# Attention in a two-layer decoder trunk: TensorE weighs the values ahead of both turnings of a step

## The reference

```python
# mixer A: 8 heads of 64, three dilated causal windows, mixed by their softmax denominators
o_a = dilated_mixture_attention(qa, ka, va)
# mixer B: 8 heads of 96 (64 + 32 rotary), values of 64, plain causal attention
s = jnp.where(k_pos[None, :] <= q_pos[:, None], s, -jnp.inf)
p = jax.nn.softmax(s, axis=-1).astype(v.dtype)
o = jnp.einsum('bhqk,bkhd->bqhd', p, v)
return jnp.concatenate([o_a, o_b], axis=-1) @ w_out
```

## Time and profile before

| | us |
|---|---|
| median of 3 runs | 2953.01 (2952.48 to 2954.64) |
| profiled execution | 2956.97 |
| its span | 2955.0 |
| attention stage in it | 263.9 to 539.4 |
| TensorE busy, whole span | 2678.8 (91%) |
| VectorE busy | 1859.8 (63%) |
| ScalarE busy | 1623.2 (55%) |
| GpSimd busy | 605.6 (20%) |

### The profile page before, as it was taken

How to read it: one execution, slowest core, us unless ns; L and a number is a source line. 1 busy time by engine, 2 the same in 40 slices (tenths; PEclk the granted TensorE clock), 3 DMA queues, 4 the chain that set the end, 5 groups by cost and what they waited for, 6 DMA issues and landing times. The chain is left out here.

```text
span 2955.0 us, 40222 instructions
## 1 busy us (share of the span) xinstructions
PE 2678.8 (91%) x13762; PEld 2149.4 (73%) x13762; DVE 1859.8 (63%) x2137; ACT 1623.2 (55%) x2050; POOL 605.6 (20%) x498
## 2 busy tenths in 40 slices
PE   7998999987999999957999997887998899999992
PEld 6885677765888787845888885765886688888771
DVE  5335766427888888865352351666453788888885
ACT  4224555324888888854232233774122688888882
POOL 0000000001343444421000001553000333333440
PEclk9998999998999999978999998888999899999996
DMA  4315110135999999952332324763214699999994
GB/s 149 88 42 169 37 44 23 36 133 188 374 378 372 373 376 371 369 222 67 102 114 76 99 86 130 275 232 140 76 36 152 235 387 384 375 372 371 366 363 194
DMA packets 306470, 618.69 MB, mean 209 GB/s; under 512 B 31832, under 2 KB 80496, under 8 KB 306224
## 3 DMA queue, kind: packets, MB, share of 16 engines
q1 hardware_dynamic: 281456, 570.94, 54.9%
q0 software_dynamic: 19136, 33.61, 3.0%
q10 hardware_dynamic: 5760, 12.59, 1.1%
HBM read 566.55 MB, written 86.13 MB: 221 GB/s over the span
## 5 line engine op out<-in xcount | busy, mean ns | idle before, releaser
L2371 DVE TENSOR_TENSOR moe_w_low<-moes_raw,moe_w_high 128x2048 fp32r<-128x2048 f32 x384 | 868.6, 2289 | 161.8 <-ACT moe_w_high L2300 161.1
L2300 ACT ACTIVATE moe_w_high<-moes_raw 128x2048 fp32r<-128x2048 f32 x384 | 725.3, 1916 | 122.6 <-PEq L150 55.7
L2167 POOL COPY moe_pick<-moes_tokens 128x1 int32 (+1 forms) x64 | 89.6, 1399 | 597.2 <-PE moe_px L2216 596.3
L174 PE MATMUL moe_pg<-moe_w_high,moe_x_high 128*128 128x512 f32 x512 | 205.9, 402 | 3.7 <-DVE moe_x_low L2421 3.7
L174 PE MATMUL moe_py<-moe_w_high,moe_h_high 128*128 128x512 f32 x512 | 209.0, 408 | 0.0
L174 PE MATMUL moe_pu<-moe_w_high,moe_x_high 128*128 128x512 f32 x512 | 204.4, 399 | 0.0
L176 PE MATMUL moe_pg<-moe_w_high,moe_x_low 128*128 128x512 f32 x512 | 202.0, 395 | 0.0
L176 PE MATMUL moe_py<-moe_w_high,moe_h_low 128*128 128x512 f32 x512 | 201.1, 393 | 0.0
L176 PE MATMUL moe_pu<-moe_w_high,moe_x_low 128*128 128x512 f32 x512 | 200.9, 392 | 0.0
L175 PE MATMUL moe_pg<-moe_w_low,moe_x_high 128*128 128x512 f32 x512 | 200.1, 391 | 0.0
L175 PE MATMUL moe_py<-moe_w_low,moe_h_high 128*128 128x512 f32 x512 | 199.5, 390 | 0.0
(11 more groups left out here) (385 smaller groups left out, 6222.5 us busy)
## 6 DMA issues: line engine op xcount, KB each, us to landing
moes_raw<-in_w_gate SPq DMA_DIRECT2D x128, 1024.0 KB, 12.4
moes_raw<-in_w_up SPq DMA_DIRECT2D x128, 1024.0 KB, 12.7
moes_raw<-in_w_down SPq DMA_DIRECT2D x128, 1024.0 KB, 12.3
sproj_raw<-in_w_in_ssd SPq DMA_DIRECT2D x40, 512.0 KB, 4.2
comb_rows<-Y SPq DMA_DIRECT2D x32, 512.0 KB, 8.8
scan_sums<-CSR SPq DMA_DIRECT2D x7, 2048.0 KB, 14.1
XC<-sproj_c SPq DMA_DIRECT2D x24, 512.0 KB, 5.1
HN<-plan_hn SPq DMA_DIRECT2D x16, 512.0 KB, 3.0
```

The lines of the kernel that those rows point to most:

```text
L174: nc.tensor.matmul(out, lh, rh, start=start, stop=False)
L2167: nc.gpsimd.tensor_copy(pick[a][:, :], M.tokens[:, bass.ds(b, 1)]).then_inc(picked[a], 1)
L2300: nc.scalar.activation(wh[c % SPLIT_SLOTS][:, :], M.raw[j][:, :], ACT.Copy).then_inc(w_high, 1)
L2371: nc.vector.tensor_tensor(wl[j][:, :], M.raw[c % RAW_SLOTS][:, :], bits(wh[j][:, :]), ALU.subtract).then_inc(w_low, 1)
```

## The change

In TensorE's order the weighing of step s - 2 moves from between the two turnings of step s - 1 to ahead of both. The orders of the other engines, the waits, the buffers and the work stay as they were.

```diff
             for s in range(NS + 2):
                 if s < NS:
                     scores(s)
-                if 1 <= s <= NS:
-                    turn(s - 1, 0)
                 if s >= 2:
                     weigh(s - 2)
                 if 1 <= s <= NS:
+                    turn(s - 1, 0)
                     turn(s - 1, 1)
```

## The result

| | before | changed |
|---|---|---|
| median of the timed runs, us | 2953.82 (2952.48 to 2955.96) | 3001.99 (2996.6 to 3004.76) |
| profiled execution, us | 2956.97 | 3003.27 |
| its span, us | 2955.0 | 3001.4 |
| attention stage in it | 263.9 to 539.5, 275.6 | 264.7 to 587.1, 322.4 |

The changed kernel is slower by a ratio of 1.0157 [1.0145, 1.0169]. The span grows by 46.4 us. The attention stage grows by 46.8, and what lies ahead of it by 0.8. The output projection behind it takes 94.7 in place of 95.8: the clock was at its lower level for 3.4 us at its start (591.0 to 594.4), before for 6.8 (542.2 to 549.0). All that follows takes 2318.8 against 2318.9. So the change costs what it costs inside the stage, as forecast; forecast were 40 us, and 46 to 48 were measured.

What follows compares the result with a forecast made beforehand. TensorE was taken to bound the attention stage. Terms of 6.3 us per first-half pair and 3.7 per second-half pair, four of each, gave +40 us and 2993 us, within a range of 2972 to 3015.

Steps and rivals of the forecast that it cites:

- likeliest case: Whole kernel: the attention stage grows by 40 us, giving 2993 us, own range 2986 to 3000; 75 in 100.
- Two signs: Attention stage: forecast wrong if the second half loses as much as the first, or the granted clock falls inside.
- TensorE sets the pace: Attention stage: TensorE busy 121.49 of 124.00 us in the first four pairs, 149.16 of 151.40 in the last; others wait.
- Late mask, kind A: First-half pairs: next scores wait for head 1's mask behind head 0's late copy; 0.72 to 0.90 us at t = 4 to 7.
- Bank wait, kind B: Second-half pairs: head 1's turning waits for a bank head 0's copy empties; 0.68, 0.79, 0.57 us at t = 5 to 7.
- The steps t = 1 to 4 lose nothing: Second-half pairs: only the bank wait remains and head 1's mask is hidden, so these steps lose 0 us.
- ScalarE's chain at t = 0: t = 0 steps: weighing waits for ScalarE's high copy behind head 1's exponential; 1.2 us first half, 1.7 second.
- Behind the last scores: End of the attention stage: the t = 0 chain comes once more without scores, about 1.8 us.
- rival D: Attention stage: the clock falls too, a half-speed spell in each first-half pair adding 24 us, 3017; 10 in 100.
- A (the bank alone, 2973): Attention stage: only the bank stalls of head 1's turning count, 2.5 us a pair, 20 in all; 8 in 100.
- C: Whole kernel: no change, 2953 us, waits of before swapped one for one; 3 in 100.
- B: Attention stage: faster, the weighing filling waits of turnings for exponentials, 7.2 us gone, 2946; 4 in 100.

Runs made afterwards that it cites:

- e3: Changed kernel with VectorE writing head 1's mask ahead of its copy of head 0's turned tiles; 2975.18 us, ratio 1.0062.
- e4: Changed kernel with three PSUM banks for turned tiles, the weighing's two result tiles becoming one; 3013.43 us, ratio 1.0190.
- e5: Kernel before with both turnings ahead of the weighing; 2984.23 us, ratio 1.0104.
- e7: Changed kernel without the weighing's wait for the finish two steps back; 3003.96 us in one execution.
- e8: Changed kernel with ScalarE copying head 1's high tiles ahead of head 1's exponential; 2992.26 us, ratio 1.0123.
- e1: Kernel before with the weighing first only in the first half of the attention stage; 2980.77 us, ratio 1.0075.
- e2: Kernel before with the weighing first only in the second half of the attention stage; 2976.75 us, ratio 1.0070.
- e9: Kernel before with head 1's mask ahead of head 0's copy (first half, t = 0 to 4) and weighing first at t = 2 to 4; 2951.50 us, 0.9981.
- e6: Kernel before with head 1's mask ahead of head 0's copy on VectorE, first half, t = 0 to 4; 2953.17 us, ratio 0.9993.

## Why the prediction was right

The direction, the place and the three mechanisms came out as said; the size was 7 us low in 47, at 1.0157 where 2993 over 2953 is 1.0135. The measured 3001.99 is within the whole range, but just above the likeliest case's own, 2986 to 3000. The shares of the halves did not come out: forecast were 23.4 and 16.6 us, measured 24.2 and 22.6, so nearly the whole miss is in the second half. Two signs that the prediction named for being wrong are therefore met or nearly so: the second half lost almost as much as the first, and the granted clock did fall inside the stage, at 577.3. Point by point:

- **TensorE sets the pace, so new holes show in full.** Right. Work stayed the same, TensorE's share of the first half fell to 81% as forecast, and nothing outside the stage took part.
- **Late mask, kind A.** Right in sign, place and size of the steps: t = 4 to 7 forecast at 0.85, 0.90, 0.81, 0.72, measured 0.87, 0.93, 0.84, 0.84. For t = 1 to 3, my estimate of 1.8 together, measured 1.86. At t = 5 to 7 it comes last by only 0.12 to 0.24 (e3), with the bank's stall right beneath it (e4). e3 recovers some 28 us; that is more than the growth of these steps, since it removes a wait that was there before too, kind B's, and part of the chain at t = 0.
- **Bank wait, kind B.** Right, and confirmed by e4 (19.3 us of it became 1.9) and e5 (it needs only the turnings side by side). The size was off: 0.79, 0.68, 0.57 forecast for t = 5 to 7, measured 1.01, 0.85, 0.73. The term "1.43 after its turning starts" is 1.53 in the rows, since VectorE's semaphore took some 0.15 us and not 0.05. Another 0.09 is the later start of the weighing behind scores of kind B. Together 0.55 a pair, 2.2 us.
- **"The steps t = 1 to 4 lose nothing" in kind B.** The one step that failed. They lose 0 + 0.23 + 0.18 + 0.11 = 0.52 a pair, 2.1 us. I had shown head 1's mask to be hidden at t = 6, and carried it to small t, where head 0's scores and head 1's turning are too short to cover it. e3 shows the cause: with the mask early all three are back at 2.47, 3.33 and 4.21.
- **ScalarE's chain at t = 0.** Right: 1.2 and 1.7 forecast, 1.26 and 1.75 measured. e7 lets the trace name it, and e8 removes its longest part at the predicted price of one exponential less a small wait.
- **Behind the last scores.** 1.8 forecast, 3.3 measured. The clock fell there for 577.3 to 580.7, so weighing and sums took 3.48 us (577.42 to 580.90) where they took 1.90 before (532.95 to 534.85): 1.6 more.
- **The clock inside the stage.** From 277 to 577 it stayed at 1.00, with 32 bank stalls of up to 0.8 us and waits of TensorE of up to 1.1 for a maximum and 1.2 for the high copy. So rival D had no part in the changed kernel but for the one spell behind the last scores, worth 1.6 us and not 24. What the Trainium skill says in "TensorE: Matmul & The Clock Gate", section "A second HAM failure mode: psum-queue depth-cycling", did not show in this pattern of short holes. Single spells of some 3.4 us, not of the 12 I had priced, came in t = 0 steps of e1, e2 and e4 and, in the changed kernel, e2 and e7, behind the last scores, where TensorE waits 1.1 to 1.8 us at once.
- **Rivals.** A (the bank alone, 2973) is close to what e3 measured when the row maximum's wait was taken away, 2975, but in the sum only: it has 2.5 us in every pair, e3 has 1.5 in kind A and 3.1 in kind B. C fell with the result, and so did B. B was also priced too high. The 7.2 us of the earlier trace rows, and the 5.4, are idle time of weight loads (PEld), not of matmuls; TensorE's holes in the whole stage were 2.51 + 2.24 us. A gain in small steps exists (e3, e9), but needs the mask to come first.

The misses add up: 2.2 for the bank's handovers, 2.1 for the small steps of kind B, 1.5 behind the last scores, and 0.8 in kind A's four pairs (24.2 against 23.4) make 6.6, which takes the 40 to 46.6 of the 46.8 measured.

## What to carry to other kernels

When an instruction moves on an in-order engine, follow what stands behind its *consumer* on the consumer's queue: here VectorE's copy became late, and with it a mask that had nothing to do with it. A buffer rotation of two is enough only as long as other work lies between two uses, and this cover has to be as long as the copy takes with its handovers (1.53 us here, from the start of the turning). Price a cover at the smallest step of a loop as well as at the largest: it was at the small ones that mine was missing, and there too that the same edit, at t = 2 to 4 of kind A and with the mask moved ahead, made a faster kernel. And where two waits end together, taking one away tells little of its price.

## What the runs showed of the hardware that was not expected

- A handover from VectorE's copy to a waiting transpose took 0.14 to 0.15 us (485.99 to 486.13), where I had counted 0.05.
- The same instructions took TensorE 2.8 us less in e9 than in e6 (266.92 against 269.75), some 1.6 of it in 12 steps whose two turnings stand together (0.12 to 0.15 each). The remainder may be the clock, which rose 2.7 us earlier in e9's execution (272.0 against 274.7). A change from one kind of matmul to another seems to have a price of its own; it was not measured by itself.
- The clock withstood 300 us with holes of 0.3 to 0.8 us in most steps. It fell around waits of 1.11 us in e1 and 1.79 behind the last scores of the changed kernel, yet not around the 1.21 us of the latter's t = 0 step at 494; in e2 a wait of the same 1.21 us in the same kind of step did bring a fall, at 428.0. So the length of one wait doesn't decide it; what does stays open.
- A wait that the trace calls "issue" can be a plain wait for another engine, when the instruction waits for several semaphores. Leaving out a redundant one named it.
